# At stage boundaries, four weight tiles go through one row block and then the other

## The reference, cut to what matters

```
for i in range(4):                       # kind A, B, C, A
    q, k, v, (qi, wi, ki,) qm = split(x @ w_in)
    mix = attention(q, k, v)             # A: only the 64 best keys by an indexer
    mk, mv = split(layer_norm(mem) @ w_mem_kv[i])
    mo = memory_attention(qm, mk, mv)    # does not depend on x
    x = layer_norm(ALPHA * x + concat(mix, mo) @ w_out[i])           # "ln1"
    x = layer_norm(ALPHA * x + swiglu(x, w_gate_up[i], w_down[i]))   # "ln2"
for i in range(2):
    h = modulated rms_norm(x)            # shift, scale, gate from a condition
    p = split(h @ w_in_2[i], 8)          # 0..3 retention q,k,v,gate; 4..7 sticks q,k,v,gate
    x = x + gate * (concat(retention, stick_breaking) @ w_out_2[i])
return rms_norm(x)
```

## Time and profile before

| | |
|---|---|
| median of 3 runs (lowest to highest) | 1826.72 us (1819.81 to 1829.87) |
| the profiled execution's own time | 1820.88 us |
| its span, first to last instruction | 1819.0 us |
| mean granted TensorE clock | 0.955 of full |
| PE, DVE, ACT busy | 1670.5, 1090.0, 743.6 us |
| transfers | 296.32 MB, mean 163 GB/s |

### The profile page before, as it was taken

One profiled execution on the slowest core, in us unless ns is written; L12 is line 12 of the kernel. 1 busy time (PEld: TensorE's weight loads), 2 busy tenths in 40 slices (PEclk: granted clock), 3 DMA queues, 4 the chain that ended last, 5 costly groups with the idle time before them and its releaser, 6 DMA issues.

```text
span 1819.0 us, 19290 instructions
## 1 busy us (share of the span) xinstructions
PE 1670.5 (92%) x7900; PEld 1348.3 (74%) x7900; DVE 1090.0 (60%) x1470; ACT 743.6 (41%) x879; POOL 45.7 (3%) x74
## 2 busy tenths in 40 slices
PE   6888899999988999998899999888999979899987
PEld 5666778878767888786688878666788858776866
DVE  4854566557566566664666557836555667456634
ACT  4434344334433334344343333443343434654372
POOL 1000000000000000000000000000000000000000
PEclk8998899999999999999899999979999989998999
DMA  8341266655324565551266555313456535233421
GB/s 299 135 139 47 93 223 221 227 200 217 116 79 153 210 242 219 208 185 47 94 230 231 208 208 208 127 59 119 168 209 236 214 110 183 107 114 126 170 88 46
DMA packets 43111, 296.32 MB, mean 163 GB/s; under 512 B 4996, under 2 KB 5124, under 8 KB 8976
## 3 DMA queue, kind: packets, MB, share of 16 engines
q1 hardware_dynamic: 38592, 279.99, 42.1%
q0 software_dynamic: 4000, 14.00, 2.4%
q10 hardware_dynamic: 432, 1.11, 0.2%
HBM read 294.03 MB, written 1.05 MB: 162 GB/s over the span
## 4 chain that ended last, share of the span: by engine, by line
PE 79%; DVE 11%; ACT 6%; issue 2%; DMA 1%; POOLq 0%; SPq 0%; DVEq 0%; ACTq 0%; POOL 0%
PE psum L605 22%; PE psum L607 22%; PE psum L606 22%; DVE w_low L1077 3%; PE psum L628 2%; PE psum L787 2%; ACT w_high L898 2%; PE psum L665 2%; ACT work L971 1%; PE psum L799 1%; PE psum L769 1%; DVE neg_max L1333 1%; PE psum L718 1%; DMA w_raw<-in_weights 1%; PE psum L860 1%
## 5 line engine op out<-in xcount | busy, mean ns | idle before, releaser
L1077 DVE TENSOR_TENSOR w_low<-w_raw,w_high 128x2048 fp32r<-128x2048 f32 x242 | 552.1, 2290 | 378.8 <-ACT w_high L898 378.5
L605 PE MATMUL psum<-w_high,xt_high 128*128 128x512 f32 (+1 forms) x1536 | 618.5, 403 | 16.6 <-DVE w_low L1077 8.6
L607 PE MATMUL psum<-w_high,xt_low 128*128 128x512 f32 (+1 forms) x1536 | 606.1, 395 | 0.0
L606 PE MATMUL psum<-w_low,xt_high 128*128 128x512 f32 (+1 forms) x1536 | 605.3, 394 | 0.0
L898 ACT ACTIVATE w_high<-w_raw 128x2048 fp32r<-128x2048 f32 x242 | 459.9, 1911 | 254.6 <-PE psum L607 248.7
L605 PEld LDWEIGHTS psum<-w_high,xt_high 128*128 128x128 f32 x1536 | 296.4, 193 | 80.6 <-issue 13.6
L607 PEld LDWEIGHTS psum<-w_high,xt_low 128*128 128x128 f32 x1536 | 295.3, 192 | 62.7
L606 PEld LDWEIGHTS psum<-w_low,xt_high 128*128 128x128 f32 x1536 | 296.4, 193 | 57.1
L605 PE MATMUL psum<-w_high,ht_high 128*128 128x512 f32 x352 | 138.2, 393 | 6.3 <-DVE ht_low L1383 6.3
L607 PE MATMUL psum<-w_high,ht_low 128*128 128x512 f32 x352 | 137.8, 391 | 0.0
L606 PE MATMUL psum<-w_low,ht_high 128*128 128x512 f32 x352 | 137.7, 391 | 0.0
(11 more groups left out here) (201 smaller groups left out, 1382.0 us busy)
## 6 DMA issues: line engine op xcount, KB each, us to landing
w_raw<-in_weights SPq DMA_DIRECT2D x266, 1024.0 KB, 4.8
norm_params<-in_ln_g POOLq DMA_DIRECT2D x8, 512.0 KB, 4.0
norm_params<-in_ln_b POOLq DMA_DIRECT2D x8, 512.0 KB, 5.3
x_rows<-in_x SPq DMA_DIRECT2D x2, 512.0 KB, 4.6
arena<-in_mem POOLq DMA_DIRECT2D x2, 512.0 KB, 19.7
norm_params<-in_norm_g POOLq DMA_DIRECT2D x2, 512.0 KB, 3.8
out_rows<-x_rows ACTq DMA_DIRECT2D x2, 512.0 KB, 2.6
mem_kv<-in_decay POOLq DMA_DIRECT2D x1, 768.0 KB, 4.8
```

Source lines behind the costliest of these rows:

```text
L605: e.matmul(dst, a_hi, b_hi, start=first, stop=False)
L606: e.matmul(dst, a_hi, b_lo, start=False, stop=False)
L607: return e.matmul(dst, a_lo, b_hi, start=False, stop=last)
L1077: e.tensor_tensor(K.w_lo[:, s, :], K.w_raw[:, r, :], K.w_hi[:, s, :].bitcast(F32), ALU.subtract).then_inc(K.taken.hit(t), 1)
```

## The change

The ring of split tiles gets five slots. A new method `group` writes two blocks (four tiles) at once: all four tiles times rb 0, then all four times rb 1, with what follows from rb 0's results (residual, norm, turned rows) placed among the products of rb 1. It is used at 21 places: the first two blocks of each later layer, projections 4 and 3 ahead of attention, `w_out`, the first two `up` steps, and in the second model projections 4 and 5, 7 and 3, and `w_out_2`. The last four `down` tiles of each feed-forward are written in the same manner, which makes 25. Splits are no longer placed by tile number: each product of rb 1 frees a slot (`owed`), and `split` takes up one that is owed. `on` is a split and one background step, after every product.

The memory keys and values of all four layers are computed in layer 0, right after the indexer's projections (`memory`); each layer's result is stored outside (`park`, 512 KB) and loaded back when its layer needs it (`load_kv`). The evacuations of layer 0's projections wait for the last store, since they write to the same memory. The second model does the sticks first and then the retention. The modulation of the second one of these layers is moved ahead of the gates of the first one. Other edits find room for the larger ring: `norm_params` has one buffer in place of two, `decay` is loaded once for each layer, and `ht_high` and `ht_low` get four buffers.

```diff
-RING = 3
+RING = 5
...
-    def split_up_to(self, t):
-        while self.split <= t:
-            self.add("split", self.split)
-            self.split += 1
+    def split(self, n=1):
+
+        for _ in range(min(n, self.owed)):
+            self.owed -= 1
+            self.add("split")
...
+    def block(self, name, layer, cols, gen, then, what="half"):
+
+        uses = [self.gemms.take() for _ in range(RB)]
+        for half in range(2):
+            t = self.tile(name, layer, cols, what, 4 * half)
+            for rb in range(RB):
+                self.gemm(t, rb, half, gen, "gemm", uses[rb])
+                if half:
+                    then(rb, uses[rb], t)
+                self.on()
+
+    def group(self, blocks, gen, after):
+
+
+        t = [[self.tile(name, layer, cols, what, 4 * half) for name, layer, cols, what, _ in blocks]
+             for half in range(2)]
+        for rb in range(RB):
+            uses = [self.gemms.take() for _ in blocks]
+            for half in range(2):
+                for n, (*_, then) in enumerate(blocks):
+                    self.gemm(t[half][n], rb, half, gen, "gemm", uses[n])
+                    if half:
+                        then(rb, uses[n], t[half][n])
+                    after[rb][2 * half + n]()
...
+    def memory(self):
+
+        for rb in range(RB):
             self.xt(("mem",), rb)
-            yield
-
-    def memory_products(self, layer):
-        uses = [self.gemms.take() for _ in range(RB)]
-        for half in range(2):
-            t = self.tile("w_mem_kv", layer, 0, "half", 4 * half)
-            self.split_up_to(t + 2)
+        for layer in range(len(KINDS)):
+            self.block("w_mem_kv", layer, 0, ("mem",), self.evacuate(("mem", layer)))
             for rb in range(RB):
-                self.gemm(t, rb, half, ("mem",), "gemm", uses[rb])
-            self.step_background()
-            yield
-        self.evacuate(("mem", layer), uses, t)
-
-    def turn_memory(self, layer):
-        for rb in range(RB):
-            self.turn("mk", layer, rb, range(2), "dve")
+                self.turn("mk", layer, rb, range(2), "dve")
+            self.add("park", layer)
+        self.add("load_kv", 0)
...
+        steps = range(FF_STEPS - 4, FF_STEPS)
+        t = {step: down_tile(step) for step in steps}
+        for rb in range(RB):
+            for step in steps:
+                down(step, t[step], rb)
+                if rb == 0:
+                    self.split()
+                    if step == FF_STEPS - 3:
+                        turn(FF_STEPS - 1)
+                elif step == FF_STEPS - 2:
+                    self.next_rows(layer, 0)
+                elif step != FF_STEPS - 1:
+                    self.split()
+            for h in range(2):
+                self.add("residual", Residual(out, rb, h, t[FF_STEPS - 1], "wide", acc[rb], h == 1))
+            self.norm(out, rb)
+            if layer == LAST:
+                self.add("rms", (0, rb))
+                self.add("modulate", (0, rb))
...
+        def attend():
+
+            self.on()
+            self.drain()
+            units = self.own_units(layer, 0)
+            first, second = [self.preceded(lambda rb=rb: self.turn("qm", layer, rb, range(2), "act"),
+                                           self.memory_unit(layer, rb)) for rb in range(RB)]
+            units = [first] + units if kind == "A" else units + [first]
+            units[-1] = self.followed(units[-1], lambda: self.xt(mix, 0))
+            self.beside(self.pipelined(units + [second] + self.own_units(layer, 1)))
...
+        self.group([proj(4), proj(3)], gen, [[self.on] * 3 + [attend], [self.on] * 4])
+        while (mix, 0, 1) not in self.xt_uses:
             self.step_background()
...
+        def rest():
+            self.split()
             self.drain()
-            self.xt(mix, 1)
-        key = ("ln1", layer)
-
-        def first_sums(uses, t):
-            for rb in range(RB):
-                self.add("residual", Residual(key, rb, 0, t, "gemm", uses[rb], True))
-        self.block("w_out", layer, 0, mix, late=late, then=first_sums)
-        uses, t = self.block("w_out", layer, BLK, mix, "wide")
+            if layer < LAST:
+                self.add("load_kv", layer + 1)
+            self.xt(mix, 1, (0,))
+
+        def end():
+            self.split()
+            self.xt(mix, 1, (1,))
+
+        def turned():
+            self.xt(("ff", layer), 0)
+            self.split()
+        self.group([("w_out", layer, h * BLK, "half", sums(h)) for h in range(2)], mix,
+                   [[self.on, self.on, rest, end], [self.split, lambda: None, turned, lambda: None]])
...
+        def gate(rb):
+            def then():
+                self.on()
+                if rb == 0:
+                    self.drain()
+                    self.add("ret_rstd", layer)
+                self.add("sb_gate", (layer, rb))
+                self.add("ret_gate", (layer, rb))
+            return then
+        self.group([proj(7), proj(3)], gen, [[self.on] * 3 + [gate(0)], [self.on] * 3 + [gate(1)]])
         self.xt(mix, 0)
...
+        if j.where[:2] == ("proj", 0):
+            act.wait_ge(*K.parked.at(len(KINDS) - 1))
...
+    def park(layer):
+        for use in plan.turns["mk", layer]:
+            pool.wait_ge(*K.tr.out(use))
+        for rb in range(RB):
+            pool.wait_ge(*K.gemms.out(plan.blocks[("mem", layer), rb]))
+        e.dma_start(K.kv_outside[layer], K.kv_made(layer)).then_inc(K.parked.hit(layer, 16), 16)
+
+    def load_kv(layer):
+        pool.wait_ge(*K.parked.at(len(KINDS) - 1))
+        if layer:
+            pool.wait_ge(*K.tr.out(plan.units[layer - 1, 1][-1].out))
+        e.dma_start(K.kv[:, :, :], K.kv_outside[layer]).then_inc(K.ld_kv.hit(layer, 16), 16)
```

More of the change, by code:

```diff
@@ L549, in second_layer, with proj, project, late @@
-        sticks[-2] = self.followed(sticks[-2], lambda: self.add("ret_gate", layer))
-        project(0, lambda: self.xt(gen, 1))
-        self.background.append(self.turn_retention(layer, 0))
+        gen, mix = ("sin", layer), ("sout", layer)
+        def proj(c):
+            return "w_in_2", layer, c * BLK, "half", self.evacuate(("proj2", layer, c), c % 4 == 3)
+        def project(c):
+            self.block(*proj(c)[:3], gen, proj(c)[-1])
+        def late():
+            self.xt(gen, 1)
+        def turn(what, rb, by):
+            def after():
+                self.split()
+                self.turn(what, layer, rb, range(4), by)
+            return after
@@ L571, in second_layer @@
-        self.block("w_out_2", layer, 0, mix, late=lambda: self.xt(mix, 1), then=first_sums)
-        uses, t = self.block("w_out_2", layer, BLK, mix, "wide")
-        for rb in range(RB):
-            self.add("add_gated", Gated(layer, rb, 1, t, "wide", uses[rb]))
+        rets = [self.retention(layer, h) for h in range(RET_H)]
+        self.beside(self.pipelined(rets))
+        if layer + 1 < DEPTH_2:
+            self.modulation(layer + 1, range(4))
+        else:
+            self.add("load_final")
@@ L576, in make, with turned @@
+        def turned():
+            if layer + 1 < DEPTH_2:
+                self.xt(("sin", layer + 1), 0)
+            else:
+                self.add("final", 0)
+            self.split()
+        self.group([("w_out_2", layer, h * BLK, "half", sums(h)) for h in range(2)], mix,
+                   [[self.split, self.split, lambda: self.xt(mix, 1), self.split],
+                    [self.split, lambda: None, turned, lambda: None]])
     def make(self):
@@ L669, in gemm @@
+        for c in range(4):
+            m = e.transpose(psum[:, K.tr.place(j.use), c * P:c * P + P], src[:, (4 * g + c) * P:(4 * g + c + 1) * P],
+                            K.ident[:, :])
+        m.then_inc(K.turned.hit(j.use), 1)
     def gemm(j):
@@ L1244, in turn @@
         dst, n = K.turn_to(j), len(j.chunks) * P
[L1245 removed]
+        v.wait_ge(*K.turned.at(plan.turns["mk", j.layer][-1] if j.what == "mk" else j.use))
         e.tensor_scalar(dst, psum[:, K.tr.place(j.use), 0:n].rearrange("p (c s) -> p c s", s=P), K.turn_scale(j.what),
```

644 lines of the change are left out of this document (314 added, 330 removed).

## The result

The changed kernel takes 1879.75 us (median of 4 runs, 1874.94 to 1880.87), the kernel before 1824.83 on the same chip; the ratio is 1.0296, 95% interval 1.0261 to 1.0331. It is slower by 3%, where a gain of 4% was forecast.

The account below looks back on a forecast made before the run. PE was taken as the bound, busy 1670.5 of 1819.0 us, so only its idle and half-rate time could be won. The terms summed to -71.5 from 1820.88, so 1749; the forecast was 1750, range 1725 to 1778.

Parts of the forecast that it names:

- the paragraph on attention: Attention units, a pipeline of nine or twelve steps: fewer steps without a product, loss from 57.6 to 26.6 us, -31.
- Layer 3's indexer: Layer 3, narrow projection to first use of chosen keys: twelve products between instead of sixteen, less cover, +5 us.
- The feed-forward: Feed-forward between boundaries: no idle time before and none after, so no term in the sum.
- Norms: Norm after w_out, four times: row block 0's chain covered by row block 1's products, 45 us becomes 2, -43.
- Boundaries: Boundary into layers 1 to 3, after the last down products: chain covered, 8.5 us becomes 0.5, -8.
- The start: Layer 0's start with all memory products: 24 us of new stalls against 12 us that go, 1 us of clock, +13.
- The stores: Storing memory keys and values outside: last store lands after 4.0 us, before its place is needed; cost nothing.
- the gates: Second model, before each w_out_2: 5.5 us idle where 3.4 stood, +4 us for two layers.
- Into the second model: Entry to the second model: idle about 9 us plus 4 by the clock, 16.8 becomes 13, -4.
- Between the two layers: Between the second model's layers: modulation leaves the path and the chain is covered, 8.2 us becomes 2, -6.
- rival 3: A group's fourth split tile comes late, 5 us at each of 25 groups gives 1875 us; chance 0.08.
- Rival 4: Stalls only move: each boundary's wait turns up one stage later, 1825 us; chance 0.05.

Follow-up runs that it names:

- narrow splits: Splits of w_out's four tiles and w_gate_up's first two per layer 64 columns wide, not 2048: changed kernel 1809.98 us, fastest complete one 1745.92; results not the reference's.
- the mended kernel: Changed kernel with background work and ada rows queued before splits, gates too, and memory evacuations of row block 1 on ACT: 1809.51 us, ratio 0.9926.
- Work before splits: Changed kernel with background work (softmax units, sticks, indexer) queued before the split that follows a product: 1834.6 us, ratio 1.0088.
- the ada order was mended: On top of Work before splits, the feed-forward's addition of ada rows queued before the split that follows the down product: 1812.97 us, ratio 0.9949.
- the kernel with splits on POOL: The mended kernel with the subtraction of six splits a layer (w_out's four tiles, w_gate_up's first two) on POOL instead of DVE: 1777.8 us, ratio 0.9746.

## Why the prediction was wrong

**The step that failed** is the paragraph on attention: "Now steps 1 to 4 and two in `w_out` have a product each: three of nine (six of twelve) are bare. If the loss goes with the bare steps". It gave -31 us. Measured from the last matmul of projection 2 to the end of `w_out` (in layer 0 of the kernel before again from the 23rd product), attention took 203.2 us beyond its products before and takes 228.3 now: it lost 25 where it was to win 31. By layer that is +3.9, +15.8, +5.8 and -0.4. I had counted the products that come between the units as pure cover, and forgot that each product of row block 1 frees a slot and is followed by a split, 1.9 us on ACT and 2.3 on DVE, in the queues on which the unit depends. I had counted DVE's queue by the instruction at the norms, at the start and at the gates, and not in the one stretch where the change put most new work. The narrow splits show that the cover itself was judged rightly: in the changed kernel they bring attention to 160.6 us, 43 below the kernel before, where 31 was forecast. That the mended kernel took 1745.9 us with them, where the prediction said 1750, is luck in good part: beside the kernel before its attention has 39 us less and its feed-forward stages 48, the start costs nothing instead of 13, and the projections of layer 3 and the second model still cost 10 and 5 us more.

**Layer 3's indexer**, +5, was put too low as well: the projections of layer 3 ahead of attention take 24.0 us beyond their products, before 6.0. PE waits 4.8 and 3.6 us there for the rotary sum and for DVE's copy of turned rows (L1300, L1319), of 12.7 us of idle time. Work before splits gives back 7.6 of the 18 us; the narrow splits, which are other tiles, nothing; the cause of the rest is open. In layer 0 the projections behind the memory products take 8.1 us, for which the sum had no term; work before splits brings them to 2.5.

**The feed-forward** "between boundaries had no idle time and has none" was wrong by 13.8 us of waits and about 15 us in all: the same mechanism, at the ada rows. The new ring is filled as far as it goes, so a split waits for the product just queued; before, with three slots and two tiles ahead, its slot was by the plan already free. I had read the depth of the ring as safety and missed that the fill level had become the full depth.

**Norms**, -43: right. The four feed-forward stages fell by 29.7 us, and by 45 once the ada order was mended. **Boundaries**, -8: the waits at the boundary into layer 1 are gone (PE's first wait after 458 ends at 477.6). But that one is 2.8 us long, for the rotary, and the projections of layers 1 and 2 are 3.4 and 1.9 us slower than before instead of 2.7 faster. With work before splits they are 1.0 and 0.9 faster.

**The start**, +13: measured +13.4. The 23rd product starts at 108.16 us before and at 121.58 now. The parts too:

```profile
43.69 0.43 PE L683 MATMUL psum<-w_high,xt_high 128*128 128x72 f32 x1 [9.51 <-DVE work L1287]
52.21 1.97 PE L741 MATMUL psum<-ident,arena 128*128 128x128 f32 x8 [1.42 <-DVE memt_low L1177]
...
95.65 0.66 PE L794 MATMUL psum<-ident,arena 128*128 128x128 f32 x2 [5.94 <-DVE arena L1287]
```

I had said 12.3 us before the memory products (10.9 by these two rows), products from about 53 (53.8), and 6.5 us in the second block (5.9). The place was off by one step: the 9.51 us stand ahead of the narrow product of row block 1, whose bank L1287 had to empty, and not ahead of the turned memory rows.

**The stores**, nothing: right. The page has `kv_outside<-arena` at 4.1 us to landing in the median of four (2.9 to 5.2), PE never waited for one, ACT once for 2.0 us: the last was issued at 126.06, 5.5 us after the last memory product ended and not 2, so the margin that I had counted on was used up. The wait for descriptors that the Trainium skill describes for transfers issued from GpSimd (page SBUF — State Buffer, section SBUF: two separate sides) did not show, though DVE was busy for 46.2 of the 70 us from 60 to 130. No run here shows whether the kind of copy that the page means ran beside a store.

**The second model.** The waits at the gates were sized well: 7.8 and 3.6 us for `xt_low` before the two `w_out_2`, forecast 5.5 each. What they replace was not: of the 3.4 us that I had read in the window at 1600, 2.5 were a wait of the sticks (PE's L860 for L1487), and the gate had 0.9. So the term was +11.7 us where +4 was forecast. Into the second model PE was idle 7.3 us with a clock of 0.91 (1496 to 1533), forecast 9 and 4 us: close. Between the two layers the stretch fell by 12.9 us, and the modulation that left it costs 8.0 where it now stands: -4.9, forecast -6. But "sticks and retention swap their stalls: nothing" failed: seven blocks of the first layer take 10.9 us more without that modulation, and those of the second 9.6. With it the model is 19 us slower where -7.5 was forecast. Work before splits gives back 10.6 of them. What the rest is, was not tried.

**The rivals.** The time of rival 3, 1875, was nearly met, but by another mechanism: PE waits for `w_low` on only two occasions after the start. Rival 4 was nearer in kind, a stall that moves, but it ended at no change. I gave 0.08 to slower, because I looked for it only at the tile that a group needs, and not at what stands behind the split.

## What to carry to other kernels

When products are moved between the steps of a chain, everything that they trigger moves along: list the refill of the ring with its engines, and look up what now stands behind it in each in-order queue. Put the refill behind the work that PE waits for, or fill the ring one slot less than it holds; here one swapped line was worth 2%, the fill level 1.3%, and both together less than either. And where no order gets the refill out of the way, give it to an engine that is idle: this was worth another 2%.

## What the hardware showed that I had not expected

POOL takes 4.57 us (24 times, 4503 to 4701 ns) for the subtraction of a 128x2048 tile that takes DVE 2.29, and it can hold DVE up meanwhile. The timeline of the kernel with splits on POOL, layer 1:

```profile
476.62 9.07 POOL L1671 TENSOR_TENSOR w_low<-w_raw,w_high 128x2048 fp32r<-128x2048 f32 x2 [15.60 <-ACT w_high L981]
...
478.98 0.69 DVE L1303 COPY arena<-psum 128x512 f32<-128x512 f32 x1 [2.12 <-PE psum L693]
...
479.65 1.69 DVE L1433 TENSOR_TENSOR work<-work 128x128 f32<-128x128 f32 x1
481.37 4.47 DVE L1435 TENSOR_TENSOR work<-work 128x128 f32<-128x128 f32 x1
485.76 0.54 DVE L1422 TENSOR_REDUCE neg_max<-psum 128x1 f32<-128x384 f32 x1
```

The sum of two 128x128 tiles takes 0.29 us elsewhere, and 4.47 us here; it ends at 485.84, POOL's second split at 485.69. Only the dilated units of layer 1 have such sums in their chain; 8.0 us of PE's waits there are for L1435, and the rest of the 14 us by which the layer stays behind I have not traced. So this layer gained nothing by the move. The copy from PSUM in the same stretch kept its 0.69 us. The Trainium skill (SBUF — State Buffer, section Who interferes with whom) states that a DVE instruction with two SBUF inputs contends with a GpSimd instruction that reads SBUF, by an exclusive lock; these rows agree.
